# Gate columns and narrow z pieces as three rounded passes, and the experts' token rows through DRAM by indirect transfers

## What is computed

```python
for i in range(DEPTH):                                  # 2 layers
    h = rms_norm(x, mix_pre_g[i])
    z = h @ w_in                                        # mixer columns, then 4 x 1024 gate columns
    # four attention branches A, B, C, D, each 256 wide, and
    gates = sigmoid(z_gate).reshape(bsz, seq, N_BRANCHES, D_MODEL)
    merged = sum(gates[:, :, n] * (o[n] @ w_branch[n]))
    x = x + rms_norm(merged @ w_out, mix_post_g[i])
    h = rms_norm(x, ffn_pre_g[i])
    # layer 0: swiglu, 4096 hidden columns; layer 1: 8 experts of 3584 hidden columns,
    # each token goes to the 2 experts with the highest logits, softmax weights
    y = swiglu(h, ...) if i % 2 == 0 else moe_swiglu(h, ...)
    x = x + rms_norm(y, ffn_post_g[i])
    x = x + rms_norm((p[i] @ ple_w_proj[i]) * sigmoid(x @ ple_w_gate[i]), ple_post_g[i])
```

## Time and profile before

| | us |
|---|---|
| median of three runs | 2053.13 (2051.37 to 2054.71) |
| profiled execution, its own time | 2061.58 |
| its span in the trace | 2059.8 |
| PE busy | 1968.7 (96 %) |
| DVE busy | 1344.1 (65 %) |
| ACT busy | 1073.9 (52 %) |
| POOL busy | 52.6 (3 %) |

### The profile page before, as it was taken

How to read it: one execution, slowest core, us unless ns; L and a number is a source line. 1 busy time by engine, 2 the same in 40 slices (tenths; PEclk the granted TensorE clock), 3 DMA queues, 4 the chain that set the end, 5 groups by cost and what they waited for, 6 DMA issues and landing times.

```text
span 2059.8 us, 26872 instructions
## 1 busy us (share of the span) xinstructions
PE 1968.7 (96%) x10030; PEld 1656.9 (80%) x10030; DVE 1344.1 (65%) x1486; ACT 1073.9 (52%) x1112; POOL 52.6 (3%) x104
## 2 busy tenths in 40 slices
PE   6999998999998999997899999999999999999986
PEld 5888887999986878886777888888788888888864
DVE  3345345555545434435678888888788888988864
ACT  4233334333325333233566776766677776777743
POOL 2100002000000100001000000000000000000000
PEclk9999999999999999998899999999999999999998
DMA  9533346555544633334698998999899999998970
GB/s 295 159 103 106 118 139 199 184 183 183 183 156 163 194 103 123 103 123 169 228 358 315 353 372 320 375 346 349 328 346 375 341 355 350 353 373 324 374 292 22
DMA packets 253439, 506.42 MB, mean 246 GB/s; under 512 B 8400, under 2 KB 90480, under 8 KB 253248
## 3 DMA queue, kind: packets, MB, share of 16 engines
q1 hardware_dynamic: 250656, 497.65, 68.2%
q0 software_dynamic: 2720, 7.91, 1.4%
HBM read 504.48 MB, written 1.05 MB: 245 GB/s over the span
## 4 chain that ended last, share of the span: by engine, by line
PE 85%; DVE 4%; DMA 4%; ACT 3%; issue 3%; POOL 0%; SPq 0%; DVEq 0%; ACTq 0%; POOLq 0%
PE ps L1042 25%; PE ps L984 17%; PE ps L1184 11%; PE ps L954 9%; PE ps L879 4%; PE ps L1127 4%; DMA ring<-in_moe_w_down_dram 3%; PE ps L857 3%; PE ps L1191 3%; PE ps L994 1%; PE ps L1003 1%; ACT down_hi_w L1387 1%; PE ps L1171 1%; PE ps L929 1%; PE ps L1023 1%
## 5 line engine op out<-in xcount | busy, mean ns | idle before, releaser
L1828 DVE TENSOR_TENSOR ring_lo<-ring,up_gate_hi_w 128x2048 fp32r<-128x2048 f32 x224 | 505.3, 2289 | 104.1 <-ACT up_gate_hi_w L1384 102.8
L1384 ACT CAST up_gate_hi_w<-ring 128x2048 fp32r<-128x2048 f32 x224 | 423.4, 1913 | 104.6 <-DMA ring<-in_moe_w_gate_dram 97.0
L1042 PE MATMUL ps<-up_gate_hi_w,tokens_hi 128*128 128x512 f32 x896 | 356.4, 398 | 1.2 <-DVE ring_lo L1828 1.2
L1042 PE MATMUL ps<-up_gate_hi_w,tokens_lo 128*128 128x512 f32 x896 | 350.7, 391 | 0.0
L1042 PE MATMUL ps<-ring_lo,tokens_hi 128*128 128x512 f32 x896 | 350.2, 391 | 0.0
L1833 DVE TENSOR_TENSOR down_lo_w<-ring,down_hi_w 128x2048 fp32r<-128x2048 f32 x112 | 256.1, 2287 | 27.9 <-ACT down_hi_w L1387 27.9
L1387 ACT CAST down_hi_w<-ring 128x2048 fp32r<-128x2048 f32 x112 | 214.4, 1915 | 56.4 <-DMA ring<-in_moe_w_down_dram 56.4
L1184 PE MATMUL ps<-hT,ring 128*128 128x256 f32 x1024 | 232.9, 380 | 0.0
L1184 PEld LDWEIGHTS ps<-hT,ring 128*128 128x128 f32 x1024 | 192.5, 190 | 27.8 <-issue 1.7
L1042 PEld LDWEIGHTS ps<-up_gate_hi_w,tokens_lo 128*128 128x128 f32 x896 | 168.9, 188 | 36.3
L1042 PEld LDWEIGHTS ps<-up_gate_hi_w,tokens_hi 128*128 128x128 f32 x896 | 169.0, 189 | 35.5 <-issue 1.6
(11 more groups left out here) (218 smaller groups left out, 2555.7 us busy)
## 6 DMA issues: line engine op xcount, KB each, us to landing
ring<-in_moe_w_gate_dram SPq DMA_DIRECT2D x112, 1024.0 KB, 5.2
ring<-in_moe_w_up_dram SPq DMA_DIRECT2D x112, 1024.0 KB, 5.2
ring<-in_moe_w_down_dram SPq DMA_DIRECT2D x112, 1024.0 KB, 8.8
ring<-in_w_in_dram SPq DMA_DIRECT2D x58, 1024.0 KB, 5.4
ring<-in_ffn_w_up_dram SPq DMA_DIRECT2D x16, 1024.0 KB, 5.4
ring<-in_ffn_w_gate_dram SPq DMA_DIRECT2D x16, 1024.0 KB, 8.0
ring<-in_ffn_w_down_dram SPq DMA_DIRECT2D x16, 1024.0 KB, 9.6
ring<-in_w_branch_dram SPq DMA_DIRECT2D x8, 1024.0 KB, 4.9
```

The costliest lines, as they stand in the source:

```text
L1042: m = mm(bank, xs[:, 4 * half + k, :], w[:, k, :], start=(half == k == n == 0), stop=(half == 1 and k == 3 and n == 2))
L1384: copy(up_gate_hi_w[:, j, :], ring[:, slot, :]).then_inc(run.up_gate_hi, 1)
L1828: v.tensor_tensor(ring_lo[:, slot, :], ring[:, slot, :], up_gate_hi_w[:, j, :], ALU.subtract)\
```

## The change

**Mixers.** The narrow z pieces (after: L1198) and the gate columns (L1256) become three rounded passes each: 48 matmuls instead of 16 float32 products for a piece, 24 instead of 8 for a unit. ACT casts the weights (`stream_his`), DVE subtracts (`stream_los`, L1775 for a narrow piece of 128 x 2048, L1778 for a gate block of 128 x 1024), both one piece or unit ahead: the low part of unit u + 1 is made at fill step u. The copies to `hT` are gone, and the work buffer is laid out anew.

**Experts.** Every expert's rows go through a DRAM buffer of 2176 rows of 4 KB. It is zeroed in layer 0. Once the ranks are known, POOL writes the token rows to their two experts' places with four indirect transfers (L874). The first expert still gathers by matmul; for each later one ACT issues a fetch of 128 rows, 512 KB, at chunk 2 of the expert before, and PE turns them by 8 transposes (L1059) at that expert's last chunk. A result is copied (`keep_result`) at chunk 1 of the next expert and stored, 512 KB, to the same rows. Scatter, spread, `y_los`, `add_back` and the later picks are gone. At the end POOL brings the results back to token order with four indirect transfers (L879), ACT and DVE weight and add them. The projection of p in layer 1 moves ahead of the experts, its 1 MB load with it.

```diff
+            def stream_his(layer, n):
+                u = n - len(NARROW_Z)
...
+                if u > 1:
+                    act.wait_ge(unit_ready, UNITS * layer + u - 1)
+                loaded(act, stream_slot(layer, n)[0])
+                if u < 0:
+                    copy(NARROW_HI[n][:, :, :], stream_full(layer, n)).then_inc(stream_hi, 1)
+                else:
+                    copy(gate_hi(u), quartered(stream_full(layer, n))).then_inc(stream_hi, 1)
...
+            def stream_los(layer, n):
+                u = n - len(NARROW_Z)
+                dve.wait_ge(stream_hi, STREAM * layer + n + 1)
...
+                    v.tensor_tensor(quartered(stream_lo(layer, n)), quartered(stream_full(layer, n)), gate_hi(u), ALU.subtract)\
+                        .then_inc(stream_split, 1)
@@ DVE, walking MIXER
+                    elif s[0] == "z":
+                        stream_los(layer, NARROW_Z.index(s[1]) + 1 if s[1] in NARROW_Z else 0)
...
                         e = egate[:, u % 2, :]
+                        if u + 1 < UNITS:
+                            stream_los(layer, len(NARROW_Z) + u + 1)
                         dve.wait_ge(egate_done, n + 1)
@@ PE, walking MIXER
                         bank = ps[:, 6 + u % 2, :]
-                        pos = WHERE[(layer, "gate", n, c // 2)]
-                        loaded(pe, pos)
-                        wg = slot_of(pos).rearrange("p (k c) -> p k c", k=NK)
+                        pe.wait_ge(stream_split, STREAM * layer + len(NARROW_Z) + u + 1)
+                        hi, lo = gate_hi(u), stream_lo(layer, len(NARROW_Z) + u)
                         for k in range(NK):
-                            mm(bank[:, 0:SEQ], wg[:, k, (c % 2) * P:(c % 2 + 1) * P], hT[:, k, :],
-                               start=(k == 0), stop=(k == NK - 1))
+                            part = hi[:, k // 4, k % 4, :]
+                            for i, (w, a) in enumerate(((part, zT_hi), (part, zT_lo), (lo[:, k, :], zT_hi))):
+                                mm(bank[:, 0:SEQ], w, a[:, k, :], start=(k == i == 0), stop=(k == NK - 1 and i == 2))
@@ SP, expert loads
                     expert_load(run, j, 0, 0, 0)
+                    if j == 1 and run is main_pass:
+                        sp.wait_ge(unit_ready, UNITS * DEPTH)
+                        sp.dma_start(proj_w, ple_w_proj[1].rearrange("(k p) c -> p k c", p=P)).then_inc(proj_in, 16)
@@ ACT, expert chunks
-            def y_his(run, e):
+            def fetch_rows(run, e):
+                act.dma_start(token_rows, by_expert[run.first_row + e]).then_inc(run.rows_in, 16)
+
+            def keep_result(run, e):
                 act.wait_ge(run.down_done, 2 * (e + 1) * E_CHUNKS)
-                activation(y_hi[:, :], acc(0).rearrange("p b c -> p (b c)"), ACT.Copy, scale=cur_g).then_inc(run.y_hi_done, 1)
+                copy(y_sb, acc(0).rearrange("p b c -> p (b c)")).then_inc(run.y_ready, 1)
+                act.wait_ge(run.y_ready, e + 1)
+                act.dma_start(by_expert[run.first_row + e], y_sb).then_inc(run.y_stored, 16)
...
                     if c == 2:
-                        routing(run, e, no_expert_before)
+                        if no_expert_before and run is main_pass:
+                            act.wait_ge(rows_scattered, 64)
+                        if not no_expert_before:
+                            act.wait_ge(run.y_stored, 16 * e)
+                        act.wait_ge(run.gathered, 2 * e + 2)
+                        fetch_rows(run, e + 1)
@@ POOL
+                if layer == 0:
+                    pool.wait_ge(rows_zero, 1)
+                    for e in range(2 * N_EXPERTS + 1):
+                        pool.dma_start(by_expert[e].rearrange("s (q c) -> s q c", q=4),
...
+                    pool.wait_ge(rows_zeroed, 16 * (2 * N_EXPERTS + 1))
+                if layer % 2:
+                    pool.wait_ge(rows_known, 1)
...
+                    pool.wait_ge(moe_done, 1)
...
```

More of the change, by code:

```diff
@@ L215, in exchange_uses @@
                 add(layer, "logits", t)
+                if t == 0:
+                    add(layer, "pt")
+                    add(layer, "proj", 0, 0)
+        else:
+            add(layer, "pt")
+            add(layer, "proj", 0, 0)
+        for t, half in ((0, 1), (1, 0), (1, 1)):
+            add(layer, "proj", t, half)
+        if layer % 2:
             add(layer, "rank")
[L217 to L220, removed]
     return {u: n for n, u in enumerate(uses)}
@@ L730, in _ @@
                         loop_ended(over_pass)
[L731 removed]
+                for pos in range(WHERE[(layer, "ple", 0)] - (layer + 1) % 2, WHERE[(layer, "ple", 3)] + 1):
                     load(pos)
@@ L986, in down_product, with turn_tokens, gather_first @@
                 return m
-            def gather(run):
+            def turn_tokens(run, e):
+                pe.wait_ge(run.rows_in, 16 * (e if run is main_pass else e + 1))
+                for half in range(2):
+                    for i in range(4):
+                        c = (4 * half + i) * P
+                        m = nc.tensor.transpose(GATHER[half][:, i * P:(i + 1) * P], token_rows[:, c:c + P], ident)
+                    m.then_inc(run.gathered, 1)
+            def gather_first(run):
+                pe.wait_ge(first_picked, 1)
                 for half in range(2):
@@ L1014, in expert_down @@
                         m.then_inc(run.down_done, 1)
[L1016 to L1025, removed]
             def expert_chunk(run):
@@ L1085, in experts, with plain_turn, plain_product @@
                 expert_down(run, last, last=True)
-                scatter(run, N_EXPERTS - 1)
-                pe.wait_ge(run.added, 2 * N_EXPERTS)
+            def plain_turn(layer):
+                pe.wait_ge(p_loaded, 32 * (layer + 1))
+                bank = bank_for(layer, "pt")
+                for k in range(2):
+                    for t in range(NT):
+                        m = nc.tensor.transpose(bank[:, k * SEQ + t * P:k * SEQ + (t + 1) * P], p_sb[:, t, k * P:(k + 1) * P], ident)
+                m.then_inc(ex_ready, 1)
+                emptied(layer, "pt")
+                if layer % 2 == 0:
+                    loaded(pe, WHERE[(layer, "proj")])
+                else:
+                    pe.wait_ge(proj_in, 16)
+            def plain_product(layer, t, half):
+                wp = slot_of(WHERE[(layer, "proj")]).rearrange("p (k c) -> p k c", k=2) if layer % 2 == 0 else proj_w
+                bank = bank_for(layer, "proj", t, half)
+                for k in range(2):
+                    m = mm(bank, pleT[:, k, t * P:(t + 1) * P], wp[:, k, half * 512:(half + 1) * 512], start=(k == 0), stop=(k == 1))
+                m.then_inc(ex_ready, 1)
             pe.wait_ge(const_in_s, 16)
@@ L1223, in _ @@
                 else:
+                    for t, half in ((0, 1), (1, 0), (1, 1)):
+                        plain_product(layer, t, half)
                     pe.wait_ge(routed, 1)
@@ L1891, in chunk @@
                         token_los(run, e, 0)
-                    if c == 1 and not no_expert_before:
-                        y_los(run, e - 1)
                     if not no_chunk_before:
@@ L1903, in chunk @@
                         expert_los(run, b, 2)
-                    if c == 1 and not no_expert_before:
-                        add_back(run, e - 1)
-                    if not split_before:
                         expert_los(run, b, 3)
```

321 lines of the change are left out of this document (178 added, 143 removed).

## The result

The changed kernel takes 2113.47 us (median of four runs, 2107.30 to 2122.66) against 2052.31 us of the kernel before in the same session: 1.030 times as long, 95 % interval 1.026 to 1.034. That is 61 us more; the forecast said 2069, and its range ended at 2112.

The account below looks back on a forecast made before the run. PE, busy 96 %, was taken as the bound, with DMA also full in the experts. Mixers +29, experts -15, start +1, end 0, zeroing +1 made +16 on 2061.6; less 8.45 to the median, 2069 us, range 2030 to 2112.

Parts of the forecast that it names:

- +29: Mixers, both layers: waits for DVE's subtract outweigh the shorter rounded products, +14.5 us a layer; ends -53 and +45.
- A +10.6: Mixers, branch A heads: second unit waits for the subtract behind softmax and rope, +5.3 us a layer.
- D +10.0: Mixers, branch D heads: three heads with a rope lose, the fourth keeps its gain, +5.0 us a layer.
- C +8.8: Mixers, branch C heads: no rope but two score sets; first and third heads lose, +4.4 us a layer.
- Zeroing, +1: Feed-forward of layer 0: writing 8.9 MB is covered by a DMA share of 0.54, +1 us (0 to +5).
- Experts, -15: Experts: half the gain taken, for one disturbed chunk (1.9 us) per expert, -15 us.
- PE's side, -35: Experts: PE drops gather and scatter, pays eight transposes, about 5 us less each; -35 us for seven experts.
- The slow way of the earlier trace: Experts' first chunks: 331 GB/s, chunks of about 18.7 us; a rival had it stay, +49, 2133 us, chance 0.12.
- The end, 0: After the experts: residual 6 us later through DRAM, but the projection's 6 us gone, 0 (-5 to +6).
- The second: Rival: mixers lose as forecast, experts give all of their 35 on PE, 2049 us; chance 0.13.
- the fourth: Rival: experts' transfers capped below 375 GB/s, an expert takes 126 us, +14, total 2098 us; chance 0.13.
- the +1 for the start: Start: projection of p moved to where PE waits for the router, find_rows and four scatters new, +1 us (-2 to +6).

Follow-up runs that it names:

- the useless matmuls: Changed kernel with 12 to 28 matmuls of no use before the wait of the second unit in heads that wait: 2093.97 us, ratio 1.0207.
- the two kernels with the experts' part alone: Changed kernel with the mixers' products as before the change: 2039.98 us; the same with zeroing transfers issued one after the other: 2028.94 us.

## Why the prediction was wrong

- **The mechanism in the mixers was right.** The second unit of a head waits for a subtract behind softmax and rope. The start after the scores (7.6 us for 7.3), the subtract's 1.22 us for 1.2 and 24 matmuls in 2.85 us for 2.88 came out; moving the subtract, with its cast, gave the heads of A and D back with interest. It was the term **+29** that was mis-sized: it measured +68. By kind, forecast and measured for both layers: A +10.6 and +20.2, D +10.0 and +22.5, C +8.8 and +19.5, tail +4.2 and +8.1, narrow pieces and branch B -4.6 and -2.0. Two things are missing in it.
- **First, the clock.** The sum treated a wait of 2 to 5 us as costing just that. After such a wait the granted clock fell to 1.2 GHz for part of the next unit in 13 of 24 heads, 4.40 us for 2.88 in the row above, and the useless matmuls put that at about 20 us. Without that, the heads of that run still stand 21.2 us a layer above the kernel before, where 14.7 was forecast. The forecast had no term for it, though it named PE waiting as the cost.
- **Second, the places where several things are late at once.** From its first unit to the next head's, the first head of A took 13.9 and 15.6 us in the two layers, forecast 11.1 + 2.4 = 13.5; the first of C 18.6 and 19.7, forecast 16.4; the third of C 14.9, forecast 12.9 (the clock is in these too); the tail +8.1 for both layers together, forecast +4.2, because not only DVE's splits of 2.29 us but ACT's cast of the same weight (1.8 us) stands before the gate's subtract: the chain there reads cast, split, subtract, unit, one after the other, which the order showed on ACT and the prediction read on DVE only.
- **Zeroing, +1, was +14.** The step that failed is "the DMA share is 0.54: that is its cover". A mean share is no cover for 8.9 MB issued at once at the stage's start, when PE had work for some 19 us in hand: it ran out at 403.7 and stood idle until 416.05. Sent one by one, the same bytes cost nothing, so the share was right and the burst was the mistake. In the window above the engines moved 361 GB/s. (The prediction also has POOL's next statistic due 90 us later. It is due after the feed-forward's last product, more than 280 us after the first of these transfers, so that this wait cost nothing.)
- **Experts, -15, were -38 in this pair of executions.** PE's side, -35, was nearer. The step that failed is the half taken off for "one disturbed chunk per expert". The trace of the changed kernel has four chunks of 18.2 to 18.7 us in all, in the first, second and last expert, and the one wait for the down weights that most experts have, after the store, costs under a microsecond. The slow way of the earlier trace rows did not settle in. The kernel before had more of it (chunks of 17.5 to 18.9 us in its first expert, and a fourth expert of 128.8 us), and its profiled execution stands 9 us above its median. So part of the 38 is luck of the pair. By the medians, the two kernels with the experts' part alone are 13.0 and 22.5 us below the kernel before; with their feed-forward (+13.4 and -0.7) and an end longer by some 6 us, that leaves about -28 to -32 for the experts, an estimate. The 358 GB/s of the Trainium skill ("DMA: Bandwidth & Descriptors", section "Where 436 GB/s comes from") does not hold as a cap for this kernel on one core: 375 GB/s over 120 us.
- **The end, 0, was +6.** The residual is later by the two trips through DRAM, 7.2 and 6.0 us, and 2.3 us of half clock came on top; the projection's 6 us did go. From the end of the last down product to the gate product 28.6 us pass, 25.1 before.
- Of the rivals none was right as a whole. The second had the experts (-35) and missed the mixers; the fourth had nearly the size (2098) for the wrong reason. Errors of +39, +13 and +6 in one direction, and of -23 and -3 (the +1 for the start, against -0.4 and -1.8 in the table) in the other, make 32 of the 44 us by which the forecast missed, with the sign right. The other 12 are that the profiled execution of before lies 8.45 us above the median used, and the changed one's 3.7 below its own. That -23 took back more than half of +39 is luck, not a merit of the sum.

## What to carry to other kernels

A faster form of an operation that needs a new preparation on another engine is worth nothing until it is known where in that engine's order the preparation stands; here the same instructions, moved by a few places, in A and D into a gap where DVE waited for ACT, turned +61 us into -40 and, with the transfers spread, -57. Cost a wait on PE with the clock that follows it, not by its length alone. Ask of a transfer not only how full the queues are on average but what else is due in the microseconds in which it is issued, and issue a long series one by one.

## What the runs showed of the hardware that was not expected

- Idle times of PE of 2.3 to 5.2 us were followed by a stretch at 1.2 GHz in 13 of 24 heads (24 matmuls in 4.2 to 5.5 us instead of 3.1 by the same rows). Three idle times of 2.7, 3.1 and 3.6 us were not. Useless matmuls in these idle times prevented it wherever they stood: 19.5 us for the whole kernel with no other change.
- Seventeen transfers of 512 KB issued at once took 17.5 us each in the median and held a 1 MB load back for 27 us; issued one after the other they took 5.0 us each, beside the same loads, which then cost the feed-forward nothing.
- An expert's extra megabyte through DRAM, on top of 44 MB of loads at a DMA share of 1.0, cost 0.5 us on average and 0.8 where no chunk was disturbed.
